# Attention written out tile by tile, bounded gathers and slot products on two column halves, in a two-block transformer kernel on one core

## The reference, cut to what matters

```
def grouped_attend(q, k, v):
    s = jnp.einsum('bkgqd,bksd->bkgqs', q, k).astype(jnp.float32) * (HEAD_DIM ** -0.5)
    p = jax.nn.softmax(s, axis=-1).astype(v.dtype)
    return jnp.einsum('bkgqs,bksd->bkgqd', p, v)
```

```
def step(out, inp):
    tok, gw, e = inp
    y = _swiglu(h[tok], wg[e], wu[e], wd[e]) * gw[:, None].astype(h.dtype)
    return out.at[tok].add(y), None
```

## Time and profile before

| | before |
|---|---|
| median of 3 runs | 4583.05 us (4575.89 to 4584.82) |
| the profiled execution | 4580.57 us |
| its span on the core | 4578.8 us |
| PE busy | 3774.5 us (82%) |
| DVE busy | 1322.5 us (29%) |
| ACT busy | 888.7 us (19%) |
| POOL busy | 374.2 us (8%) |

### The profile page before, as it was taken

One profiled execution on the slowest core, in us unless ns is written; L12 is line 12 of the kernel. 1 busy time (PEld: TensorE's weight loads), 2 busy tenths in 40 slices (PEclk: granted clock), 3 DMA queues, 4 the chain that ended last, 5 costly groups with the idle time before them and its releaser, 6 DMA issues. The chain is left out here.

```text
span 4578.8 us, 60007 instructions
## 1 busy us (share of the span) xinstructions
PE 3774.5 (82%) x23936; PEld 2258.1 (49%) x23936; DVE 1322.5 (29%) x2849; ACT 888.7 (19%) x1711; POOL 374.2 (8%) x463
## 2 busy tenths in 40 slices
PE   4698569999999756899999659969667779999975
PEld 1254345555555323444445349955365445555543
DVE  0000442222101253222117654440155332222222
ACT  0100331111001123111001233311233212222211
POOL 2000000000000000000000120000000013333331
PEclk7799679999999868999999769989855789999997
DMA  9710001111111000122121000001000259999996
GB/s 388 335 51 29 3 32 46 51 51 51 47 51 50 24 23 0 44 76 78 69 83 46 9 2 4 4 18 60 18 2 23 105 181 331 337 336 334 338 354 241
DMA packets 97929, 494.94 MB, mean 108 GB/s; under 512 B 12736, under 2 KB 17760, under 8 KB 66896
## 3 DMA queue, kind: packets, MB, share of 16 engines
q1 hardware_dynamic: 74928, 435.93, 26.1%
q0 software_dynamic: 22816, 56.31, 5.1%
HBM read 454.44 MB, written 37.75 MB: 107 GB/s over the span
## 5 line engine op out<-in xcount | busy, mean ns | idle before, releaser
L438 PE MATMUL psum<-arena 128*128 128x512 f32 x2112 | 1019.5, 599 | 52.1 <-PEq L1050 29.1
L536 PE MATMUL psum<-arena 128*128 128x512 f32 x1408 | 665.1, 594 | 4.2 <-ACT arena L376 4.2
L438 PEld LDWEIGHTS psum<-arena 128*128 128x128 f32 x2112 | 402.8, 191 | 323.3 <-issue 280.0
L2539 PE MATMUL psum<-arena 128*64 128x256 f32 x3072 | 356.1, 379 | 47.1 <-DMA arena<-exp_w_in 45.3
L536 PEld LDWEIGHTS psum<-arena 128*128 128x128 f32 x1408 | 266.7, 190 | 194.9 <-issue 174.4
L440 PEld LDWEIGHTS psum<-arena 128*128 128x128 f32 x1168 | 221.8, 190 | 283.9 <-issue 283.9
L440 PE MATMUL psum<-arena 128*128 128x256 f32 x1168 | 349.2, 379 | 0.0
L2539 PEld LDWEIGHTS psum<-arena 128*64 128x64 f32 x3072 | 212.6, 134 | 219.7 <-DMA arena<-exp_w_in 63.5
L564 DVE SCALAR_TENSOR_TENSOR arena<-psum,arena 128x511 f32<-128x511 f32 (+1 forms) x132 | 83.2, 658 | 553.5 <-ACT arena L548 553.5
L538 PEld LDWEIGHTS psum<-arena 128*128 128x128 f32 x704 | 133.1, 189 | 169.6 <-issue 169.6
L538 PE MATMUL psum<-arena 128*128 128x256 f32 x704 | 209.6, 378 | 0.0
(11 more groups left out here) (432 smaller groups left out, 4589.7 us busy)
## 6 DMA issues: line engine op xcount, KB each, us to landing
arena<-exp_w_in SPq DMA_DIRECT2D x207, 1024.0 KB, 18.7
arena<-w_mod_r_in SPq DMA_DIRECT2D x18, 4096.0 KB
arena<-w_ffn_up_in SPq DMA_DIRECT2D x88, 512.0 KB, 3.5
arena<-w_ffn_down_in SPq DMA_DIRECT2D x16, 1408.0 KB, 5.9
arena<-w_in_in SPq DMA_DIRECT2D x35, 512.0 KB, 3.6
arena<-w_even_in_in SPq DMA_DIRECT2D x17, 512.0 KB, 3.5
arena<-w_qkv_in SPq DMA_DIRECT2D x12, 512.0 KB, 3.8
arena<-acc SPq DMA_DIRECT2D x12, 512.0 KB, 8.6
```

Of the source, the lines that this page charges most:

```text
L438: mm = pe.matmul(ps[:, 2 * b, :], lhsT, src[:, k, 0:LAT], start=(k == 0), stop=(k == kt - 1))
L536: mm = pe.matmul(ps[:, 2 * b, :], lhsT, A[:, k, 0:LAT], start=(k == 0), stop=(k == KD - 1))
L2539: mm = pe.matmul(ps[64 * c:64 * c + 64, 0, 0:256], xt[u][:, k, :], wgu[w][:, k, :, c * P:(c + 1) * P], start=(k == 0), stop=(k == KD - 1))
```

## The change

In the attention the loops are gone and 32 tiles are written out in one row. The scores run two tiles ahead, also across heads; the products with the values are made tile by tile, 128 columns each, one tile behind the transposes; the softmax tile has three places in SBUF and not two, the turned tile two, and the output two PSUM banks. The copy of the queries (`qs`) is gone. In the experts the gather names a bound, so that it leaves out numbers over 511; the 128 rows of zeros in `h2` and the DMA that wrote them are gone; the three places that gathers write are cleared once by DVE (`xz`). `slots_of` makes its products in two column halves of 64.

```
@@ attention, tensor
-                    for j in range(TT):
-                        mm = pe.matmul(ps[:, 6, :], vt[:, kv, j, :], pt[:, j, :], start=(j == 0), stop=(j == TT - 1))
-                    mm.then_inc(s["pv"], 1)
+            def scores(g):
+                if g >= 2:
+                    pe.wait_ge(s["ex"], g - 1)
+                b = 2 * (g % 2)
+                lhsT, k = qkv[:, g // 4, g % 4 * P:(g % 4 + 1) * P], qkv[:, 8 + g // 16, :]
+                pe.matmul(ps[:, b, :], lhsT, k[:, 0:LAT], start=True, stop=True)
+                pe.matmul(ps[:, b + 1, 0:CTX], lhsT, k[:, LAT:T], start=True, stop=True).then_inc(s["sco"], 1)
+
+            def values(g):
+                n, t = g // 4, g % 4
+                pe.wait_ge(s["ptc"], g + 1)
+                if t == 0 and n >= 2:
+                    pe.wait_ge(s["oe"], n - 1)
+                for j in range(TT):
+                    mm = pe.matmul(ps[:, 6 + n % 2, t * P:(t + 1) * P], vt[:, n // 4, j, :], pt[:, g % 2, j, :],
+                                   start=(j == 0), stop=(j == TT - 1))
+                mm.then_inc(s["pv"], 1)
+
+            scores(0)
+            scores(1)
+            for g in range(N):
+                if g + 2 < N:
+                    scores(g + 2)
+                pe.wait_ge(s["pn"], g + 1)
+                if g:
+                    pe.wait_ge(s["ptc"], g)
+                for j in range(TT):
+                    mm = pe.transpose(ps[:, 4 + j // 4, (j % 4) * P:(j % 4 + 1) * P], pr[:, g % 3, j * P:(j + 1) * P], m["ident"])
+                mm.then_inc(s["tr"], 1)
+                if g:
+                    values(g - 1)
+            values(N - 1)
@@ attention, scalar
+            for g in range(N):
+                act.wait_ge(s["nm"], g + 1)
+                if g >= 3:
+                    act.wait_ge(s["tr"], g - 2)
+                act.activation(pr[:, g % 3, :], pair_banks(ps, g % 2, T), ACT.Exp, scale=scale, bias=sm[:, g % 3, 0:1],
+                               accum_out=sm[:, g % 3, 3:4]).then_inc(s["ex"], 1)
+                if g:
+                    turned(g - 1)
+                if g % 4 == 2 and g > 4:
+                    done(g // 4 - 1)
@@ attention, vector
-                    dve.tensor_scalar(qs, flat[:, bass.ds(i * T + kv * 4 * T, LAT)], 1.0, None, MUL).then_inc(s["q"], 1)
+            for g in range(N):
+                maxima(g)
+                if g:
+                    weights(g - 1)
+            weights(N - 1)
@@ router, sync
-            sp.dma_start(io["h2"][LAT:ROWS, :], zero).then_inc(s["st"], 16)
@@ experts
-        for t in range(4):
-            mm = pe.matmul(ps[:, 6, 0:4], onehot[:, t, :], pick[:, t, :], start=(t == 0), stop=(t == 3))
+        for t in range(4):
+            for c in range(2):
+                mm = pe.matmul(ps[64 * c:64 * c + 64, 6, 0:4], onehot[:, t, 64 * c:64 * c + 64], pick[:, t, :],
+                               start=(t == 0), stop=(t == 3))
-                                        bass.IndirectOffsetOnAxis(ap=idg[0:64, u:u + 1].bitcast(U32), axis=0)
-                                        ).then_inc(s[f"ga{u}"], 16)
+                                        bass.IndirectOffsetOnAxis(ap=idg[0:64, u:u + 1].bitcast(U32), axis=0),
+                                        bounds_check=LAT - 1, oob_is_err=False).then_inc(s[f"ga{u}"], 16)
+            dve.memset(at(BIG + NS * EW, NS * D), 0.0).then_inc(s["xz"], 1)
```

More of the change, by code:

```diff
@@ L1200, in attention @@
 def attention(nc, m, io, then):
-    st, s = stage(nc, "att", "q sco mx nm ex own pn tr ptc pv oe")
+    st, s = stage(nc, "att", "sco mx nm ex rs pn tr ptc pv oe")
     at, ps = m["at"], m["ps"]
     qkv = at(BIG, 12, T)
-    flat = at(BIG, 12 * T)
     vt = at(AT_V, 2, TT, P)
     o = AT_S
[L1208 to L1213, removed]
+    pr, o = at(o, 3, T), o + 3 * T
+    pt, o = at(o, 2, TT, P), o + 2 * T
+    sm, o = at(o, 3, 4), o + 12
     scale = float(P) ** -0.5
+    N = 32
     with st, nc.Block() as block:
@@ new lines, in turned, with done @@
+            def turned(g):
+                act.wait_ge(s["tr"], g + 1)
+                if g >= 2:
+                    act.wait_ge(s["pv"], g - 1)
+                act.activation(pt[:, g % 2, :, :].rearrange("p j c -> p (j c)"), pair_banks(ps, 2, T), ACT.Copy
+                               ).then_inc(s["ptc"], 1)
+            def done(n):
+                act.wait_ge(s["pv"], 4 * n + 4)
+                act.activation(m["A"][:, n, 0:LAT], ps[:, 6 + n % 2, :], ACT.Copy).then_inc(s["oe"], 1)
+            for g in range(N):
[8 more added lines that the diff above has]
+                    done(g // 4 - 1)
@@ new lines, in maxima, with weights @@
+            def maxima(g):
+                dve.wait_ge(s["sco"], g + 1)
+                if g >= 3:
+                    dve.wait_ge(s["ex"], g - 2)
+                    dve.wait_ge(s["pn"], g - 2)
+                x = sm[:, g % 3, :]
+                dve.tensor_reduce(x[:, 2:3], pair_banks(ps, g % 2, T), AX.X, ALU.max).then_inc(s["mx"], 1)
+                dve.wait_ge(s["mx"], g + 1)
+                dve.tensor_scalar(x[:, 0:1], x[:, 2:3], -scale, None, MUL).then_inc(s["nm"], 1)
+            def weights(g):
+                x = sm[:, g % 3, :]
+                dve.wait_ge(s["ex"], g + 1)
+                dve.reciprocal(x[:, 1:2], x[:, 3:4]).then_inc(s["rs"], 1)
+                dve.wait_ge(s["rs"], g + 1)
+                dve.tensor_scalar(pr[:, g % 3, :], pr[:, g % 3, :], x[:, 1:2], None, MUL).then_inc(s["pn"], 1)
```

61 lines of the change are left out of this document (9 added, 52 removed).

## The result

The changed kernel takes 4439.4 us (median of 4 runs, 4434.3 to 4447.5) against 4580.6 us of the kernel before on the same chip: a ratio of 0.969, interval 0.9678 to 0.9703. It is 141 us faster.

A forecast was written before the change was run, and what follows sets the result against it. The prediction took the attention as a chain and the experts as bound by DMA. 4580.6 - 95 - 23 - 2 = 4460.6 us profiled, or 4463 against the median, with a range of 4442 to 4493.

The forecast's parts named there:

- What bounds the kernel: Attention: a chain with no engine full; experts: DMA sets the end, by 0.4 us and 3.0 us a block over PE.
- Attention, -95 us: Attention stage falls from 204.7 to 110 us, at 3.3 us of PE work a tile; bounds -101 and -82.
- The clock: Attention: PE, as dense as in the experts, runs at the full 2.4 GHz from the first transposes on.
- Rivals 2 and 4: Attention: clock stays at 0.80, 4489 us, 7 in 100; order doesn't overlap as summed, 4476 to 4495, 8 in 100.
- rival 4: Attention: waits for a place in each tile spoil the overlap, 13 to 32 us more; 8 in 100.
- Gathers, -23 us: Experts: 2048 empty rows, 8.39 MB, no longer fetched, priced like weight reads at 2.78 us for a MB.
- The two rows that I set aside: Experts' gathers: other prices, 37 us by the software queue's 4.36 for a MB, 40 by half a gather-scatter pair.
- Slot products, -2 us: Experts: halves run side by side in 0.5 to 0.8 us, worth nothing in the blocks, 2 us at the stage's start.
- Rival 3: Experts: the two halves of the slot products wait for one another, 250 us more, 4713 us; 3 in 100.
- cover for the gathers' term: Experts: PE's period falls to some 6.9 us, leaving room behind DMA for the gathers' saving.
- At nothing: Start of the experts: DVE's clearing of 2.9 us hides in a wait of 4.99 us for the tables.
- Rival 1: Experts: left-out gather rows give no time, since the engines with the first rows keep their work; 4486 us, 35 in 100.

The follow-up runs named there:

- att_only: The kernel before with only the new attention and the clearing of the gathers' places; 4481.8 us, ratio 0.9784.
- att_one_ahead: The changed kernel with attention scores running one tile ahead and not two; 4549.6 us, ratio 0.9924.
- after_again: The changed kernel itself, run once more beside the scatter experiments; 4442.3 us, ratio 0.9694.
- gather_only: The kernel before with only the bounded gathers, attention and slot products as they were; 4536.4 us, ratio 0.9901.
- slots_only: The kernel before with only the slot products on column halves, plus the clearing; 4578.5 us, ratio 0.9991.
- no_slots: The changed kernel with the slot products back in one piece of 128 columns; 4443.1 us, ratio 0.9706.
- third_end: The changed kernel with empty slots gathered whole and the last 22 of every block's 64 slots left out; 4463.6 us.
- rows_third: The changed kernel with empty slots gathered whole and every third slot of each block left out, 2178 rows; 4441.5 us.
- rows_high: The changed kernel with empty slots gathered whole and slots 32 to 63 of every block left out; 4403.9 us.
- rows_odd: The changed kernel with empty slots gathered whole and every second slot of each block left out; 4405.9 us.

## Why the prediction came out as it did

**What bounds the kernel: right.** The attention was a chain with PE idle and the experts were DMA's, as the three single parts show: a shorter PE block gives nothing in the experts and fewer bytes do.

**Attention, -95 us: right.** The stage took 109.3 us from its first matmul, against a forecast of 110, and -95.4 against -95. The tile's parts were forecast as 1.29, 0.72 and 1.32 and measured as 1.29, 0.66 and 1.34. By whole runs, att_only gives 98.2; that is the stage, the copy of the queries and the spread of the medians. The clock, the assumption on which the term stood, was 0.98. The Trainium skill, TensorE: Matmul & The Clock Gate, Part 4, does not count transposes as busy for the clock; here a fifth of PE's work is transposes and the granted clock does not suffer from it, so the trace decides against using that sentence for this stage. Of transposes by themselves no run here says anything. Rivals 2 and 4 fall with it. att_one_ahead shows the part of rival 4 that was real: the waits that it feared come at a look-ahead of one, and then with the clock's fall on top.

**Gathers, -23 us: the step that failed, as a mis-sized term.** The mechanism was right: 9.17 MB less in the software queue, DMA still full, the window shorter. The step was "A gather is a read as the weights are, so I take the nearest": it priced the left-out rows by their own bytes at the weights' 2.78 us for a MB, and put at nothing what their absence does to the other queue. Measured are 37.5 us in the window of the two profiles, 39.3 for after_again against att_only, 44.0 for gather_only against slots_only (777.6 - 733.6) and 43.7 in gather_only's time: 1.1 to 1.3 us for 64 rows of 4 KB, or 4.1 to 4.8 us for a MB. The queues' shares in the window say where it lies: the software queue's packets took 27 us less, 3.2 us for a MB and so near the price taken, and the weights' packets, the same bytes, 18 us less. gather_only against att_only shows the same two amounts (30 and 21). That these packets got shorter is seen; why is not shown. The two rows that I set aside gave 37 us (the software queue's 4.36 us for a MB) and 40 (half of the pair, 1.25 us). Both come near the measured term, and both by luck: the first counts the gathers' own packets too dear (4.36 against 3.2) and leaves the weights' out, and the second halves a pair that is not split equally, 1.2 to the gather and 0.65 to the scatter, 1.85 together against the 2.5 from which it came. The count of rows was short by 192 too, which is 2 us of the term at the price I used.

With the measured 37.5 in its place the sum is 4580.6 - 95.4 - 37.5 - 2 = 4445.7, and the untouched stages' 2.4 us bring it to 4443.3, against 4442.7 profiled. So of the 23.6 us between the forecast of 4463 and the median of 4439.4, the gathers are 14.5 and the untouched stages 2.4. Another 5.7 are how the profiled executions lie to their medians: the forecast added 2.4 for it, and the changed kernel's profiled execution lies 3.3 over its median.

**Slot products, -2 us: right.** They took 0.64 us of the forecast 0.5 to 0.8, and showed nothing in the blocks. The medians can't tell the term (1.6 us in slots_only, 3.7 between no_slots and the change), but the start of the stage does: it is 2.6 us shorter in the profiles with the halves. A row of that start (the products of 1.87 us at the low clock in the earlier trace rows now take 1.02):

```profile
3616.51 1.02 PE L2411 MATMUL psum<-arena 128*64 128x4 f32 x16 [2.30 <-DVE arena L2613]
```

Rival 3, halves that wait for one another, is refuted by the 0.64. The prediction said that the shorter block is "cover for the gathers' term". It was not needed: gather_only, with the slot products as they were, has a window of 733.6, against 735.6 and 737.7 of the changed kernel.

**At nothing: right.** The clearing takes 2.6 us and stands where DVE waited for its tables anyway:

```profile
3604.36 2.62 DVE L2605 MEMSET arena<- 128x3072 f32 x1 [1.93 <-PEq L2129]
3607.32 0.17 DVE L2612 COPY arena<-arena 128x8 f32 x1 [0.34 <-issue]
```

**Rival 1** was given 35 in 100 on the ground that nothing says which engine moves which row. That no time is gained is refuted. third_end against rows_third shows that its worry had a core: 22 rows at a gather's end are worth less than 22 spread ones, with the engines less full. The Trainium skill, DMA: Bandwidth & Descriptors, in its part on why a DMA increments its semaphore by 16, gives runs of neighbours for direct copies; if that held for these gathers and the fullest engine set the end, rows_high would have given nothing and rows_odd everything. They gave 79 and 74 us, so these runs speak against using that rule for indirect ones.

**The range** ended at 4442 because it joined the upper gathers' price, 17 us, with 4 us of the attention, though the attention's own bound of -101 was 6 better than its term; that would have made 4440. It left nothing for other executions' spread, although the runs of before alone lie 9 us apart, and nothing for stages that the change does not touch.

## What to carry to other kernels

Where DMA bounds a stage, do not price a transfer that goes away by its own bytes alone: look what the other queue's packets take beside it. And price the two directions apart: here 64 gathered rows of 4 KB were worth 1.2 us, of which their own packets were some 0.8, and the same bytes scattered with an add 0.65, though their own packets took 1.2. Before shortening an engine's block, look which wait grows when it is shorter: 0.4 us a block showed nothing behind DMA and 27 us in 96 blocks once DMA had been relieved. In a pipeline of tiles, count the look-ahead by the length of the chain beside it, and count a missing step twice, for the idle time and for the clock that PE loses with it.

## What the runs showed of the hardware that was not expected

A gathered row that is left out by its bound stays in the queue as a packet under 512 bytes. The queue's count of packets is the same to the one (22816), and about 1.2 us for 64 rows are saved all the same. The end gains more than the rows' own packets took: the weights' packets beside them, the same 211 MB, took 558 us of all 16 engines instead of 577.

What a left-out row saves depends on which and how many are left out with it: from 0.40 us for 64 (the last 22 of every gather) over 1.03 (22 spread ones) to 1.4 to 1.6 (any half). The two kernels with 22 rows left out have the same packets, bytes and packet time, and the one that takes 21 us longer has the DMA share at 0.99 and not 1.02. Why is not settled.

A stage of which a fifth is transposes ran at a granted clock of 0.98 with PE busy 98%, and the same instructions with 1.97 us of idle time in nearly every tile at 0.79, in 218 us instead of 110.
